# A removal key's norm moved into the projection that makes the key, and low-rank products on row halves

## The reference, cut to what matters

```python
def _rwkv_branch(z, mu, w0, w2, a0, a2, g2, k_k, k_a, r_k, ln_g, S0):
    zc = z[..., OFF_C:]                                   # 12 blocks of 128 columns
    zc = zc + mu * (0.5 * (_shift_prev(zc) + _shift_next(zc)) - zc)
    r, k, v, dw, da, dg = jnp.split(zc, C_SPLITS, axis=-1)
    dw = jnp.tanh(dw.reshape(bsz, t, N_DIR, DECAY_RANK))
    ...
    a = jax.nn.sigmoid(a0 + jnp.einsum('btrj,rjc->btrc', da.reshape(bsz, t, N_DIR, ICLR_RANK), a2))
    g = jax.nn.sigmoid(dg) @ g2
    kk = (k * k_k).astype(f32).reshape(bsz, t, C_H, C_N)
    kk = kk / jnp.maximum(jnp.linalg.norm(kk, axis=-1, keepdims=True), 1e-12)
```

## Time and profile before

| what | value |
|---|---|
| median of three runs | 2052.94 us (2051.46 to 2055.0) |
| the profiled execution's own time | 2050.03 us |
| its span on the core | 2048.3 us |
| mean granted TensorE clock | 0.952 |
| busy: TensorE | 1858.0 us (91%) |
| busy: VectorE | 1048.8 us (51%) |
| busy: GpSimd | 738.7 us (36%) |
| busy: ScalarE | 604.5 us (30%) |

### The profile page before, as it was taken

How to read it: one execution, slowest core, us unless ns; L and a number is a source line. 1 busy time by engine, 2 the same in 40 slices (tenths; PEclk the granted TensorE clock), 3 DMA queues, 4 the chain that set the end, 5 groups by cost and what they waited for, 6 DMA issues and landing times. The chain is left out here.

```text
span 2048.3 us, 48154 instructions
## 1 busy us (share of the span) xinstructions
PE 1858.0 (91%) x20004; PEld 1755.1 (86%) x20004; DVE 1048.8 (51%) x1964; ACT 604.5 (30%) x1362; POOL 738.7 (36%) x522
## 2 busy tenths in 40 slices
PE   6989997789974899999966998999999999999997
PEld 5979996579963787888845998999999999999997
DVE  7218535877247666667576245343434343434344
ACT  6311133332244555555423222020202020101122
POOL 3223242434332233223343513434343444343433
PEclk8999998899987999999967999999999999999998
DMA  9741012211300000000022201111111111111113
GB/s 366 237 146 42 23 42 80 67 35 42 99 18 5 7 4 4 4 4 3 4 83 103 62 11 37 47 37 46 38 51 33 51 31 51 32 50 36 46 37 118
DMA packets 145950, 114.23 MB, mean 56 GB/s; under 512 B 13018, under 2 KB 130289, under 8 KB 145021
## 3 DMA queue, kind: packets, MB, share of 16 engines
q1 hardware_dynamic: 145536, 111.79, 17.5%
q10 hardware_dynamic: 253, 0.08, 0.0%
HBM read 99.01 MB, written 12.84 MB: 55 GB/s over the span
## 5 line engine op out<-in xcount | busy, mean ns | idle before, releaser
L502 PE MATMUL bank<-YT_r,Z_r 128*128 128x384 f32 x2304 | 402.6, 335 | 3.2 <-DVE YT_r L2993 3.2
L502 PEld LDWEIGHTS bank<-YT_r,Z_r 128*128 128x128 f32 x2304 | 398.9, 188 | 5.9 <-issue 5.0
L2648 DVE SCALAR_TENSOR_TENSOR XT<-bank,MOD,XT 128x384 f32 (+5 forms) x288 | 142.3, 515 | 320.9 <-PE bank L502 318.5
L502 PE MATMUL bank<-HT_r,W_r 128*128 128x384 f32 x1296 | 258.2, 341 | 4.4 <-PEq L111 4.4
L502 PEld LDWEIGHTS bank<-HT_r,W_r 128*128 128x128 f32 x1296 | 230.8, 190 | 6.0 <-issue 5.4
L2949 ACT ACTIVATE PAD<-PAD,up_bias 128x384 f32<-128x384 f32 (+2 forms) x128 | 65.2, 533 | 554.5 <-DVE PAD L2987 554.5
L480 POOL TENSOR_TENSOR Z_r<-Z,ones 128x512 fp32r<-128x512 f32 x64 | 87.8, 1372 | 297.6 <-DMA Z<-in_mlp_w 297.6
L480 POOL TENSOR_TENSOR W_r<-Z,ones 128x1024 fp32r<-128x1024 f32 x32 | 78.2, 2444 | 197.3 <-DMA Z<-in_mlp_w 197.1
L502 PE MATMUL bank<-Z_r,W_r 128*128 128x388 f32 (+1 forms) x720 | 139.8, 336 | 2.1 <-POOL Z_r L486 2.1
L502 PE MATMUL bank<-Z_r 128*128 128x388 f32 (+1 forms) x720 | 140.1, 337 | 0.0
L502 PEld LDWEIGHTS bank<-Z_r,W_r 128*128 128x128 f32 x720 | 126.1, 188 | 2.4 <-POOL Z_r L486 2.4
(11 more groups left out here) (426 smaller groups left out, 3356.4 us busy)
## 6 DMA issues: line engine op xcount, KB each, us to landing
Z<-in_w_mod SPq DMA_DIRECT2D x12, 2048.0 KB, 13.3
Z<-in_mlp_w SPq DMA_DIRECT2D x32, 512.0 KB, 4.4
Z<-in_mlp_w SPq DMA_DIRECT2D x64, 256.0 KB, 2.8
YT<-gate_rows_x SPq DMA_DIRECT2D x18, 384.0 KB, 4.0
YT<-in_w_in SPq DMA_DIRECT2D x12, 512.0 KB, 3.8
PAD<-in_w_in SPq DMA_DIRECT2D x10, 512.0 KB, 4.6
XT<-residual SPq DMA_DIRECT2D x1, 4608.0 KB, 13.5
out<-HT SPq DMA_DIRECT2D x9, 512.0 KB, 2.7
```

Of the source, the lines that this page charges most:

```text
L502: mm = nc.tensor.matmul(out, w[slot][:, k, :], x(k, g), start=(n == 0 and k == 0), stop=(n == 2 and k == self.blocks - 1))
L2648: ins = nc.vector.scalar_tensor_tensor(out=x, in0=S.PS[3 * slot + g][:, a:b], scalar=S.MOD[:, ds(col, 1), c:c + 1].rearrange("p a b -> p ( ...
```

## The change

Four things are done.

The slabs come in another order, `ORDER_C = (3, 4, 5, 6, 7, 8, 10, 9, 11, 0, 1, 2)`: k first, then v, the low-rank blocks, and r last.

The removal key's norm moves from `prepare_c` into the second half of `project_c`, whose loop is written out. VectorE scales all three pairs when the first half is mixed (`scale_k_dve`). ScalarE squares one pair at a time into one buffer (`square_act`). TensorE sums the squares in two parts, two groups into banks 6 and 7 and then the third group into bank 6 again (`sum_pe`, `PARTS`), at fixed places: ahead of units 2 and 4 for the first pair, 8 and 10 for the second, 14 and 16 for the third (`SUMS` counts from 0). VectorE copies the sums out with a maximum of 1e-24 (`clip_dve`); ScalarE takes logarithm and exp(-0.5 x) (`root_act`) in place of root and reciprocal; VectorE multiplies by -kk in place (`negate_dve`). Tanh and sigmoid of blocks 9 and 11 move to ScalarE's place behind the drain of unit 14. SyncE loads A2 without padding at the end of `project_c`.

The low-rank products use only the 64 rows of their direction, of weights and of input, go direction by direction within a pair, and alternate between banks 0 to 2 and 3 to 5.

The masks are made by GpSimd in the first stage, ahead of a conversion that waits for a load there. `nkk` stays where the scaled key was made, and the buffers that lay there move to another area.

```diff
@@ begin, GpSimd @@
             nc.gpsimd.memset(WG, 0.0).then_inc(gate_cleared.sem, 1)
+            for b in range(2):
+                r = slice(N * b, N * b + N)
+                one(nc.gpsimd.tensor_copy(S.block_ident[r, :], S.ident[r, r]))
+                ...
             pool.wait_ge(gate_loaded.sem, gate_loaded.at())
             nc.gpsimd.tensor_copy(WH_r, WG).then_inc(gate_high.sem, 1)
@@ project_c @@
+    kkr, sq = [S.YT[:, 5 + p, :] for p in range(NP)], S.PAD[2][:, 0:T]
+    S.rwkv_a2 = A2 = S.YT[:, 0, 0:C_W]
+    SUMS = {1: (0, 0), 3: (0, 1), 7: (1, 0), 9: (1, 1), 13: (2, 0), 15: (2, 1)}
+    PARTS = (((0, 6), (1, 7)), ((2, 6),))
+    def scale_k_dve(dve):
+        dve.wait_ge(mixed.sem, mixed.at(EARLY - 1, 2))
+        for p in range(NP):
+            nc.vector.tensor_scalar(kkr[p], S.Z[:, 3 + p, :], S.param("rwkv_k_k", p, 1), None, ALU.mult).then_inc(
+                scaled.sem, 1)
+    def square_act(act, p):
+        act.wait_ge(scaled.sem, scaled.at(0, p + 1))
+        if p:
+            act.wait_ge(negated.sem, negated.at(0, p))
+        nc.scalar.activation(sq, kkr[p], ACT.Square).then_inc(squared.sem, 1)
+    def sum_pe(pe, p, part):
+        pe.wait_ge(squared.sem, squared.at(0, p + 1))
+        if p or part:
+            pe.wait_ge(clipped.sem, clipped.at(0, 2 * p + part))
+        else:
+            pe.wait_ge(stored.sem, stored.at(NT - 1))
+        for g, bank in PARTS[part]:
+            mm = nc.tensor.matmul(S.PS[bank][:, 0:GRP], S.halves[:, :], sq[:, g * GRP:(g + 1) * GRP], start=True, stop=True)
+        mm.then_inc(summed.sem, 1)
+    def clip_dve(dve, p, part):
+        dve.wait_ge(summed.sem, summed.at(0, 2 * p + part + 1))
+        for g, bank in PARTS[part]:
+            ins = nc.vector.tensor_scalar(sq[:, g * GRP:(g + 1) * GRP], S.PS[bank][:, 0:GRP], 1e-24, None, ALU.max)
+        ins.then_inc(clipped.sem, 1)
+    def root_act(act, p):
+        act.wait_ge(clipped.sem, clipped.at(0, 2 * p + 2))
+        nc.scalar.activation(sq, sq, ACT.Ln).then_inc(logged.sem, 1)
+        act.wait_ge(logged.sem, logged.at(0, p + 1))
+        nc.scalar.activation(sq, sq, ACT.Exp, scale=-0.5).then_inc(rooted.sem, 1)
+    def negate_dve(dve, p):
+        dve.wait_ge(rooted.sem, rooted.at(0, p + 1))
+        dve.wait_ge(scaled.sem, scaled.at(0, p + 1))
+        nc.vector.scalar_tensor_tensor(out=kkr[p], in0=kkr[p], scalar=-1.0, in1=sq, op0=ALU.mult,
+                                       op1=ALU.mult).then_inc(negated.sem, 1)
@@ project_c, SyncE @@
+            for d in range(2):
+                sp.dma_start(A2[N * d:N * d + N, :], io["rwkv_a2"][0, d]).then_inc(a2_loaded.sem, 16)
@@ project_c, TensorE @@
-            with pe.Fori(EARLY, 6) as i:
-                for slot in range(2):
-                    dense.multiply(pe, i, slot, group(S.HTr), group(S.XTr))
+            for s, (i, slot) in enumerate(LATE):
+                def with_sums(g, s=s):
+                    if 3 * s + g in SUMS:
+                        sum_pe(pe, *SUMS[3 * s + g])
+                dense.multiply(pe, i, slot, group(S.HTr), group(S.XTr), with_sums)
@@ project_c, ScalarE @@
-            with act.Fori(EARLY, 6) as i:
-                for slot in range(2):
-                    act.wait_ge(mixed.sem, mixed.last(i, slot + 1))
-                    for g in range(NG):
-                        own_act(act, i, slot, g)
-            act.wait_ge(mixed.sem, mixed.at(5))
-            nc.scalar.activation(S.Z[:, 9, :], S.Z[:, 9, :], ACT.Tanh)
-            nc.scalar.activation(S.Z[:, 11, :], S.Z[:, 11, :], ACT.Sigmoid)
+            square_act(act, 0)
+            for s, (i, slot) in enumerate(LATE):
+                act.wait_ge(mixed.sem, mixed.last(i, slot + 1))
+                for g in range(NG):
+                    own_act(act, i, slot, g)
+                    if 3 * s + g in (4, 10, 16):
+                        root_act(act, (3 * s + g) // 6)
+                    if 3 * s + g in (5, 11):
+                        square_act(act, (3 * s + g + 1) // 6)
+                    if 3 * s + g == 13:
+                        act.wait_ge(mixed.sem, mixed.at(4, 1))
+                        nc.scalar.activation(S.Z[:, 9, :], S.Z[:, 9, :], ACT.Tanh)
+                        nc.scalar.activation(S.Z[:, 11, :], S.Z[:, 11, :], ACT.Sigmoid)
@@ prepare_c, TensorE @@
-            for d in range(2):
-                for p in range(NP):
-                    ...
-                        mm = nc.tensor.matmul(S.PS[3 + g][:, 0:GRP], C.A2[:, d, p * P:(p + 1) * P],
-                                              S.Z[:, 10, g * GRP:(g + 1) * GRP], start=True, stop=True)
+            for n, (p, d) in enumerate(ORDER):
+                if n >= 2:
+                    pe.wait_ge(a_done.sem, a_done.at(0, n - 1))
+                r = slice(N * d, N * d + N)
+                for g in range(NG):
+                    mm = nc.tensor.matmul(S.PS[3 * d + g][:, 0:GRP], A2[r, p * P:(p + 1) * P],
+                                          S.Z[r, 10, g * GRP:(g + 1) * GRP], start=True, stop=True)
```

More of the change, by code:

```diff
@@ L799, in _, with one @@
             nc.gpsimd.memset(WG, 0.0).then_inc(gate_cleared.sem, 1)
+            masks = S.flag("levels_made")
+            n_masks = 0
+            def one(ins):
+                nonlocal n_masks
+                ins.then_inc(masks.sem, 1)
+                n_masks += 1
+                pool.wait_ge(masks.sem, masks.at(0, n_masks))
+            for b in range(2):
+                r = slice(N * b, N * b + N)
+                one(nc.gpsimd.tensor_copy(S.block_ident[r, :], S.ident[r, r]))
+                for d in range(2):
+                    one(nc.gpsimd.tensor_copy(S.block_tri[r, d, :], S.tri["UPS" if d == 0 else "LOS"][r, r]))
+            for d in range(2):
+                for i in range(LEVELS - 1):
+                    b = 1 << i
+                    m = S.whole_level[:, :].rearrange("p (n h x) -> p n h x", h=2, x=b)
+                    src = m[:, :, d, :]
+                    one(nc.gpsimd.memset(S.whole_level[:, :], 0.0))
+                    one(nc.gpsimd.memset(src, 1.0))
+                    first = b if d == 0 else 0
+                    for base, mult, step in ((-first, 1, -2 * b), (first + b - 1, -1, 2 * b)):
+                        one(nc.gpsimd.affine_select(out=src, in_=src, compare_op=ALU.is_ge, fill=0.0, base=base,
+                                                    pattern=[[step, P // (2 * b)], [0, b]], channel_multiplier=mult))
+                    for half in range(2):
+                        r = slice(N * half, N * half + N)
+                        one(nc.gpsimd.tensor_copy(S.block_level[r, d, i, :], S.whole_level[r, r]))
             pool.wait_ge(gate_loaded.sem, gate_loaded.at())
@@ L1533, in _ @@
                 if 4 <= r < 6:
-                    dense.load(sp, 0, r - 4, w_in[:, :, OFF_C + (r - 4) * P:OFF_C + (r - 3) * P])
+                    at = OFF_C + ORDER_C[r - 4] * P
+                    dense.load(sp, 0, r - 4, w_in[:, :, at:at + P])
                 if 9 <= r < 11:
@@ L1612, in project_c @@
     SLABS = [(i, slot) for i in range(EARLY) for slot in range(2)]
+    LATE = [(i, slot) for i in range(EARLY, 6) for slot in range(2)]
+    kkr, sq = [S.YT[:, 5 + p, :] for p in range(NP)], S.PAD[2][:, 0:T]
+    S.rwkv_a2 = A2 = S.YT[:, 0, 0:C_W]
+    scaled, squared, summed = S.flag("ck_scaled", NP), S.flag("ck_squared", NP), S.flag("ck_summed", 2 * NP)
+    clipped, logged, rooted = S.flag("ck_clipped", 2 * NP), S.flag("ck_logged", NP), S.flag("ck_rooted", NP)
+    negated = S.flag("ck_negated", NP)
@@ L1684, in _ @@
             sp.wait_ge(ab_saved.sem, ab_saved.at())
+            for d in range(2):
+                sp.dma_start(A2[N * d:N * d + N, :], io["rwkv_a2"][0, d]).then_inc(a2_loaded.sem, 16)
+            sp.wait_ge(a2_loaded.sem, a2_loaded.at())
         @block.tensor
@@ L1733, in _ @@
                 mix_dve(dve, i, slot)
-            with dve.Fori(EARLY, 6) as i:
-                for slot in range(2):
-                    mix_dve(dve, i, slot)
+            scale_k_dve(dve)
+            mix_dve(dve, *LATE[0])
+            for part in range(2):
+                clip_dve(dve, 0, part)
+            negate_dve(dve, 0)
+            for p in range(1, NP):
+                mix_dve(dve, *LATE[2 * p - 1])
+                if p == 1:
+                    mix_dve(dve, *LATE[2])
+                    clip_dve(dve, 1, 0)
+                else:
+                    clip_dve(dve, 2, 0)
+                    mix_dve(dve, *LATE[4])
+                clip_dve(dve, p, 1)
+                negate_dve(dve, p)
+            mix_dve(dve, *LATE[5])
+ORDER_C = (3, 4, 5, 6, 7, 8, 10, 9, 11, 0, 1, 2)
 class StoreC:
@@ L1791, in prepare_c @@
     nc, io = S.nc, S.io
-    kkr = [S.YT[:, 5 + p, :] for p in range(NP)]
-    sq = [S.PAD[p][:, 0:T] for p in range(NP)]
-    loaded, cleared = S.flag("cp_loads", 16 * 4), S.flag("cp_cleared", 2)
-    squared, summed, rooted = S.flag("cp_squared", NP), S.flag("cp_summed", NP), S.flag("cp_rooted", NP)
```

(18 more changed lines are left out.)

85 lines of the change are left out of this document (18 added, 67 removed).

## The result

| | before | after |
|---|---|---|
| median of 19 runs each | 2051.2 us | 2057.2 us |
| ratio (95% interval) | | 1.0031 (1.0023 to 1.0039) |
| span of the profiled execution | 2048.3 us | 2052.5 us |
| mean granted TensorE clock | 0.952 | 0.942 |
| busy: TensorE | 1858.0 us | 1864.4 us |

The change makes the kernel slower by 0.31%, 6.4 us of 2051. The forecast was 2057.2.

The account below looks back on a forecast made before the run. TensorE was taken to bound the projection's second half, VectorE's chain and the low-rank products the preparation. Second half +28.0, tail -1.6, preparation -22.3, masks +0.2 gave +4.3 us, 2057.2 on the median; range 2050.5 to 2060.5.

Parts of the forecast that it names:

- Second half: Third projection's second half: 103.2 us instead of 75.18, 28.0 more, from sums, three TensorE waits and clock loss.
- The three waits: Projection's second half: TensorE idles 4.3 us ahead of unit 2, 5.5 ahead of unit 4, 5.5 ahead of unit 10.
- The sums: Projection's second half: nine matmuls of two passes add 6.1 us on a full TensorE.
- the 6.6 taken: Projection's second half: TensorE's clock loss after idling, 2.2 us for each of three waits.
- First wait: Ahead of unit 2: scaling held until GpSimd's first split ends, 4.3 us; rival of no hold 2.2, chance 0.11.
- Tail: Between the projection's last unit and the next stage: 6.8 us instead of 8.40.
- Preparation: Stage after the tail: 16.6 us instead of 38.89, paced by TensorE's six low-rank products.
- 2.2 us for half clock: Preparation: added because TensorE comes to the low-rank products after some 7 us of idling.
- the rival of overlapping products: Preparation: low-rank products on different row halves run beside each other, 14.1 us instead of 16.6; chance 0.10.
- Their sum: Whole kernel: 28.0 - 1.6 - 22.3 + 0.2 = +4.3 us, 2057.2 on the median.
- The 0.2 for the masks in the first stage: First stage: masks moved to GpSimd's gap cost 0.2 us, between 0 and 0.5, as VectorE and GpSimd hold each other up.
- The rival "the norm is hidden": Projection's second half: second and third wait don't exist if clip precedes mix on VectorE; -11.1 us, 2041.8; chance 0.07.

Follow-up runs that it names:

- the version without waits: Changed kernel with the clip ahead of the mix for the first two pairs and the first two sums ahead of unit 3 instead of 2: 2033.82 us.
- sums_later: Changed kernel with only the first two sums moved, ahead of unit 3 instead of unit 2: 2049.9 us.

## Why the prediction was right, step by step

- **Second half**, forecast 103.2, measured 101.79. The three waits were where the order put them, 4.14 + 5.24 + 5.24 = 14.6 us against 4.3 + 5.5 + 5.5, and none stood ahead of units 8, 14 and 16. The sums cost 6.2 (the version without waits). The clock cost less than the 6.6 taken: from the restart to the second group of eight matmuls 4.43 us (520.38 to 524.81) for what takes 2.75, and 3.94 and 3.86 for 2.07, 5.3 in all. Some 0.4 us of the stage is in none of these.
- **First wait.** That the scaling is held until GpSimd's split ends was the choice between two rows; it was the right one (2.8 us for the first scaling, 0.76 a scaling without the split).
- **Tail**, forecast 6.8, measured 6.51.
- **Preparation**, forecast 16.6, measured 18.89, just inside the 19 above which the prediction would have called itself wrong: the term that was most off, through the clock. I had added 2.2 us for half clock, as behind a short wait; a mean clock of 0.59 means that TensorE was at half for 82% of the stage, 15 us. The clock rose only at about 629.9, and at about 633.3 it fell again while the products went on (the last three lines below, by the view of the earlier trace rows). Serial passes at that clock would have made it longer still, but the rival of overlapping products was half true: the first twelve passes lasted 5.62 us where the earlier trace rows has 4.21 for six, so a run on one half does overlap the next run on the other, which I had denied.

```profile
620.23 5.62 PE L1920 MATMUL bank<-Z,YT 64*128 64x384 f32 x12 [6.55 <-PEq L1745]
```

```profile
629.00:630.00 1.00, 1.00 (x5) 0.58 (x3) 0.00 (x0) 0.00 (x0) 0.00 (x0) 0.56 0.00 0
632.00:633.00 1.00, 1.00 (x4) 0.58 (x4) 0.00 (x0) 1.00 (x3) 0.00 (x0) 1.00 0.00 0
633.00:634.00 1.00, 1.00 (x5) 0.56 (x4) 0.00 (x0) 0.09 (x1) 0.00 (x0) 0.64 0.00 0
```

- **Their sum.** The errors of the second half (-1.4), the tail (-0.3) and the preparation (+2.3) nearly cancel: 4.3 forecast, +4.7 in the three stages, 4.2 in the span. The medians differ by 6.0 and the ratio by 6.4 (4.7 to 8.0); a forecast of 0.21% stood at the border of what can be told, and the measured 0.31% lies beyond it. That the median is met to 0.1 us is luck: the difference forecast is 4.3 and the medians differ by 6.0, but the forecast was put on the 2052.94 of three runs of the kernel before, and the median of 19 is 2051.2. The 0.2 for the masks in the first stage can't be told from the spread named below.
- **The rival "the norm is hidden"** failed by two rows of VectorE's order, as its condition said; with them exchanged the second half gives back 14.6 us.

Open: by which moment the chip raises the clock again. After one wait of 5.24 us the loss was 1.9 us in the changed kernel and 2.5 or more in `sums_later`, where the waits and the instructions behind them are the same. And parts of the program that are the same in these kernels, or nearly so, differ between single traces: the second half starts between 511.9 and 518.0 us in the changed kernel and its variants, and what follows the preparation lasts from 1411.0 to 1416.7. A single span can't price a step of a few us, a stage's length can.

## What to carry to other kernels

Work that is moved under a full engine must have every wait of that engine followed back through the queue of the one who ends it: here a clip of 1 us stood behind a mix that itself waited for the full engine's last result, and the gain of 20 us in one stage was paid for by 26 in the stage that gave cover. Read the order of the instructions on the releasing engine, and put the short step on which the full engine waits ahead of the long one on which nobody does. Where two chains of a stage end together, or a function brings a table load, a part of a change tried alone can lose what the whole gains.
